# A third of the convolution on GpSimd during attention, the large gate halves on VectorE, the convolution's norm at the seventh gate and its columns ahead of the last gate's third product

## The chip, the cores and the metric

The kernel runs on one core of one Trainium2 chip. The metric is the device time of one execution in microseconds (us); lower is better. The engines are named as the profile names them: PE is TensorE (PEld its weight loads), DVE is VectorE, ACT is ScalarE, POOL is GpSimd, SP is SyncE, which here only issues loads.

## The reference, cut to what matters

Two layers of a trunk run on 512 latent and 128 context tokens, all in fp32. In each layer a normalised input `u` is projected to q, k, v, to the input of a convolution module, and to two gates. Attention and convolution are two branches, merged by the gates:

```python
proj = u @ w_in
q, k, v, a_glu, gates = jnp.split(proj, ...)
attn_br = block_attention(q, keys, vals) @ w_attn_o
ga, gb = jnp.split(a_glu, 2, axis=-1)
cv = depthwise_conv(ga * jax.nn.sigmoid(gb), conv_w, conv_b)      # 31 taps, 512 channels
cv = jax.nn.silu(layernorm(cv, conv_ln_g, conv_ln_b))
conv_br = cv @ w_conv_o
gate_a, gate_c = jnp.split(gates, 2, axis=-1)
merged = jax.nn.sigmoid(gate_a) * attn_br + jax.nn.sigmoid(gate_c) * conv_br
h = h + g1 * (merged @ w_out)
```

A mixture of 16 experts follows in each layer, then the next layer.

## The kernel before, in words

Every engine has its own program, written out in order; semaphores tie them together, and nothing reorders the work. Both layers run the same loop body, so each stage stands twice in the trace.

Products are exact to fp32 by splitting: a number is written as a high half (rounded, type fp32r) and a low half (the rest), and each product is three passes on PE, high x high, high x low, low x high. For a weight tile that SP has loaded into `raw`, ACT writes the high half `w_hi` (function `hi`, L1097) and POOL subtracts it to get the low half `w_lo` (function `lo` of GpSimd, L2261). There are two slots of each; a tile is 128 x 2048 or 128 x 1024.

Tokens stand in 640 columns. The stages of a layer around the change are:

* GLU: the input of the convolution, `glu`, four chunks of 128 channels by 700 columns (pads included). It ends before attention.
* Attention: 16 heads, taken in pairs. For each pair DVE computes the inverse row sums (`rinv`, L1667), POOL spreads them into `rrow` (L2301, function `inverse_row`), and PE turns them (L615, function `inverse_rows`) one pair of heads later. POOL also sends three rows of the modulation to memory (`modulation`, `bias`), and has nothing else there.
* Gates: eight gates (`b8` 0 to 7). Each has three products of 48 matmuls of 320 columns: `gta` and `gtc` (both from one tile of 128 x 2048, the "large half" below is its `w_lo`) and `ao` (the attention output, a tile of 128 x 1024), all at L534. ACT takes the sigmoids of the first two (`sga` L1315, `sgc` L1321), DVE multiplies `ao` by `sga` into `m_t` (L1843). Beside this DVE runs the convolution: 31 taps by four chunks, 124 instructions of 128 x 670, four TENSOR_SCALAR (L1832) and 120 SCALAR_TENSOR_TENSOR (L1835), 21 per gate in gates 0 to 4 and 19 in gate 5, going round the four chunks, so that an instruction depends on the fourth one before it. They stand in DVE's program ahead of the two `m_t` of their gate.
* The convolution's norm: ahead of gate 7 PE transposes the convolution to tokens (L711, `conv_tokens`), DVE takes mean and variance and writes `cn` (L1810 to L1822, `conv_norm`), and ACT takes a square root between. After gate 7 PE transposes `cn` back to channels (L734), ACT applies SiLU (L1331) and takes the high half (L1333), DVE the low half `c_lo` (L1857).
* co: the product with `w_conv_o` (L534 again, 192 matmuls), which waits for the last `c_lo`; DVE merges it (L1870, L1873) and splits the result (`m_lo`, L1861); the product with `w_out` (L791) waits for the last `m_lo`.

Of the kernel before, what the change touches and what calls it, by code (L numbers as in the profile page):

```python
# [164 lines left out]
def _build(nc, io, out, ledger, ctx):  # L165
# [64 lines left out]
    cv = at("cv", [P, CCH, CO], F32, R_A + 60 * KB)  # L230
# [66 lines left out]
    n1row = at("n1row", [P, 512], F32, R_W + 20 * KB)  # L297
# [67 lines left out]
    wrow = routed("wrow", [P, 1], F32)  # L365

# [63 lines left out]
    def _(eng):  # L430
# [37 lines left out]
        with eng.Fori(0, DEPTH) as l:  # L468
# [235 lines left out]
            def conv_tokens():  # L704

                eng.wait_ge(*T.at("cv"))
                for t in range(NT):
                    b = fill(("cvT", t))
                    c0 = t * P if t < LT else CTX0
                    for c in range(CCH):  # L710
                        ins = nc.tensor.transpose(ps[:, b, c * P:(c + 1) * P], cv[:, c, c0:c0 + P], ident[:, :])  # L711
                    ins.then_inc(*T.filled(("cvT", t)))


            for b8 in range(KC):
# [12 lines left out]

            eng.wait_ge(*T.at("cn"))
            for c in range(CCH):  # L730
                for part, tiles in ((0, range(LT)), (1, (LT,))):
                    b = fill(("cT", c, part))
                    for i, t in enumerate(tiles):
                        ins = nc.tensor.transpose(ps[:, b, i * P:(i + 1) * P], cn[:, t, c * P:(c + 1) * P], ident[:, :])  # L734
                    ins.then_inc(*T.filled(("cT", c, part)))
# [339 lines left out]
    def _(eng):  # L1075
# [8 lines left out]
        with eng.Fori(0, DEPTH) as l:  # L1084
# [220 lines left out]

            for b8 in range(KC):
                if b8 == KC - 1:
# [17 lines left out]
            for c in range(CCH):
                if c >= 2:
                    eng.wait_ge(*A.at("c_lo", c - 2))
                for part, (c0, n) in enumerate(((0, NLAT), (NLAT, P))):
                    eng.wait_ge(*A.at("filled", ("cT", c, part)))
                    b = A.bank(("cT", c, part))  # L1330
                    act(c_f[:, c % 2, c0:c0 + n], ps[:, b, 0:n], ACT.Silu, bias=lnb[:, c:c + 1], scale=lng[:, c:c + 1]).then_inc(*A.drained(("cT", c, part)))  # L1331
                eng.wait_ge(*A.at("drained", ("cT", c, 1)))
                act(c_hi[:, c, :], c_f[:, c % 2, :], ACT.Copy).then_inc(*A.up("a_c", "c_hi", c))  # L1333
# [106 lines left out]
    def _(eng):  # L1440
# [30 lines left out]
        with eng.Fori(0, DEPTH) as l:  # L1471
            V.l = l

            def lo(n):

                eng.wait_ge(*V.at("w_hi", n))
                if n < U_MOE:
# [5 lines left out]
                    v.tensor_tensor(w_of(n, 0), raw[:, n % 2, :], w_of(n, 1).bitcast(F32), ALU.subtract).then_inc(*V.up("v_lo", "w_lo", n))  # L1483
# [317 lines left out]
            taps = [(k, c) for k in range(TAPS) for c in range(CCH)]  # L1801
            tap_step = {}
            share = -(-len(taps) // (KC - 2))
# [23 lines left out]

            for b8 in range(KC):
                for k, c in taps[b8 * share:(b8 + 1) * share]:
                    src = glu[:, c, k:k + CO]  # L1830
                    if k == 0:
                        ins = v.tensor_scalar(cv[:, c, :], src, convw[:, c, 0:1], convb[:, c:c + 1], ALU.mult, ALU.add)  # L1832
                    else:
                        eng.wait_ge(*V.at("v", tap_step[(k - 1, c)]))
                        ins = v.scalar_tensor_tensor(out=cv[:, c, :], in0=src, scalar=convw[:, c, k:k + 1], in1=cv[:, c, :],  # L1835
                                                     op0=ALU.mult, op1=ALU.add)
                    ins.then_inc(*V.step())
                    tap_step[(k, c)] = V.steps
# [5 lines left out]
                if b8 == KC - 2:  # L1844
                    ALIAS(("cv",), ("v", tap_step[(TAPS - 1, CCH - 1)]))
                    conv_norm()
# [330 lines left out]
    def _(eng):  # L2177
# [70 lines left out]
        with eng.Fori(0, DEPTH) as l:  # L2248
# [76 lines left out]
            for n in range(U_GATE + 2, U_MOE):  # L2325
                lo(n)
# [138 lines left out]
```

## Time and profile before

| | us |
|---|---|
| median of 3 runs (1926.95 to 1933.87) | 1927.54 |
| the profiled execution's own time | 1929.48 |
| its span, first to last instruction | 1927.6 |
| busy PE / DVE / POOL | 1581.1 / 1257.6 / 616.8 |
| mean granted TensorE clock, as a share of full speed | 0.909 |

All rows come from the one profiled execution; it took 1.9 us more than the median. A busy PE is not PE at its peak: matmuls are pipelined, and a matmul of 320 columns that is listed with 0.31 us starts 0.147 us after the one before. Where rows say "x2" or more, instructions that follow each other closely are put in one row. What stands in brackets at a row's end is the idle time of the engine before it, and whom it waited for.

### The profile page before, as it was taken

To read this page: it belongs to the slowest core of one execution; us is meant where nothing else is said; L and a number is where in the kernel's file an instruction comes from. 1 tells how busy PE (TensorE), PEld (TensorE's weight loads), DVE (VectorE), ACT (ScalarE), POOL (GpSimd) and SP (SyncE) were. 2 spreads that over 40 slices of the span, in tenths; PEclk is the share of its full clock that TensorE was granted. 3 is DMA by queue.
4 is the path that set the end of the run, shared out by engine and by line. 5 is a ranking of instruction groups with operands and counts; after the bars stand their busy time and mean duration, and the time that the engine had idled before them with its cause. 6 is when DMAs were issued, how large, how long until landed. Compare 5 with 4: busy or idle time off the path is not lost.

```text
span 1927.6 us, 26921 instructions
## 1 busy us (share of the span) xinstructions
PE 1581.1 (82%) x8954; PEld 1352.6 (70%) x8954; DVE 1257.6 (65%) x1728; ACT 785.0 (41%) x1178; POOL 616.8 (32%) x298
## 2 busy tenths in 40 slices
PE   2799899879998894999649989998899889399970
PEld 0589766669998673777538976667899878377750
DVE  0658588888844454778284948887984355568735
ACT  0413477731123131666142247775111322266621
POOL 2123100053322210789312320003333221059941
PEclk7799899989998895999869999999999989599995
DMA  7513165222221615799862205541222162569976
GB/s 280 195 44 93 52 210 179 78 57 65 69 64 47 259 74 187 276 357 366 300 214 71 66 29 197 187 132 34 66 67 66 45 239 70 221 227 363 369 290 228
DMA packets 131202, 310.02 MB, mean 161 GB/s; under 512 B 11636, under 2 KB 81396, under 8 KB 109984
## 3 DMA queue, kind: packets, MB, share of 16 engines
q1 hardware_dynamic: 104096, 224.41, 33.9%
q0 software_dynamic: 16400, 42.90, 6.1%
q10 hardware_dynamic: 10560, 40.90, 5.6%
q8 instruction: 76, 1.25, 0.3%
q14 instruction: 70, 0.57, 0.1%
HBM read 287.06 MB, written 39.44 MB: 169 GB/s over the span
## 4 chain that ended last, share of the span: by engine, by line
PE 50%; issue 16%; DMA 13%; DVE 11%; POOL 6%; ACT 4%; DVEq 0%; ACTq 0%; POOLq 0%; SPq 0%
PE ps L534 15%; PE ps L493 9%; PE ps L791 6%; POOL w_lo L2261 4%; PE ps L592 3%; DMA raw<-in_w_down 3%; PE ps L602 2%; DVE gu_lo L1485 2%; PE ps L449 2%; DMA raw_x<-in_w_down 2%; DMA raw<-in_w_ada 2%; PE ps L857 2%; PE ps L581 2%; PE ps L837 1%; DMA raw_x<-in_w_up 1%
## 5 line engine op out<-in xcount | busy, mean ns | idle before, releaser
L2261 POOL TENSOR_TENSOR w_lo<-raw,w_hi 128x2048 fp32r<-128x2048 f32 (+1 forms) x60 | 259.9, 4336 | 516.7 <-ACT w_hi L1097 516.5
L534 PE MATMUL ps<-u_hi,w_hi 128*128 128x320 f32 x768 | 245.5, 320 | 35.4 <-POOL w_lo L2261 29.7
L534 PE MATMUL ps<-u_lo,w_hi 128*128 128x320 f32 x768 | 242.6, 316 | 0.0
L534 PE MATMUL ps<-u_hi,w_lo 128*128 128x320 f32 x768 | 242.4, 316 | 0.0
L1835 DVE SCALAR_TENSOR_TENSOR cv<-glu,convw,cv 128x670 f32<-128x670 f32 x240 | 235.8, 1057 | 0.0
L1097 ACT ACTIVATE w_hi<-raw 128x2048 fp32r<-128x2048 f32 (+1 forms) x64 | 101.3, 1591 | 310.2 <-PE ps L534 151.1
L534 PEld LDWEIGHTS ps<-u_hi,w_hi 128*128 128x128 f32 x768 | 149.1, 194 | 39.1 <-issue 16.7
L534 PEld LDWEIGHTS ps<-u_lo,w_hi 128*128 128x128 f32 x768 | 149.5, 195 | 0.1
L534 PEld LDWEIGHTS ps<-u_hi,w_lo 128*128 128x128 f32 x768 | 149.0, 194 | 0.0
L2340 POOL DMA_INDIRECT xe<-u_d,tab_u x34 | 77.7, 2286 | 179.4 <-issue 145.7
L1700 DVE TENSOR_TENSOR pt_lo<-ps,pt_hi 128x512 fp32r<-128x512 f32 x160 | 109.7, 687 | 31.2 <-ACT pt_hi L1222 29.1
L1661 DVE TENSOR_REDUCE nmax<-ps 128x1 f32<-128x640 f32 x128 | 104.0, 815 | 27.6 <-PE ps L582 25.9
L1196 ACT ACTIVATE probs<-ps,nmax 128x640 f32<-128x640 f32 x128 | 101.4, 793 | 49.6 <-DVE nmax L1661 47.1
L592 PEld LDWEIGHTS ps<-ident,probs 128*128 128x128 f32 x640 | 77.6, 144 | 62.2 <-issue 32.8
L1222 ACT ACTIVATE pt_hi<-ps 128x512 fp32r<-128x512 f32 x160 | 94.8, 594 | 54.2 <-PE ps L592 46.2
L592 PE MATMUL ps<-ident,probs 128*128 128x128 f32 x640 | 102.3, 284 | 17.0 <-DVE pt_lo L1700 9.1
L837 PE MATMUL ps<-gu_hi,xt_hi 128*128 128x512 f32 x240 | 96.8, 403 | 19.9 <-DVE xt_lo L2091 19.8
L2301 POOL COPY rrow<-rinv 128x512 f32<-128x512 f32 x16 | 9.8, 613 | 295.7 <-DVE rinv L1667 295.7
L837 PE MATMUL ps<-gu_lo,xt_hi 128*128 128x512 f32 x240 | 94.0, 392 | 0.0
L837 PE MATMUL ps<-gu_hi,xt_lo 128*128 128x512 f32 x240 | 93.5, 389 | 0.0
L581 PE MATMUL ps<-k_hi,q_st 128*128 128x320 f32 x256 | 85.3, 342 | 5.1 <-DVE q_st L1631 1.7
L791 PE MATMUL ps<-w_hi,m_hi 128*128 128x512 f32 x160 | 65.8, 411 | 18.3 <-DVE m_lo L1861 18.3
(372 smaller groups left out, 4121.1 us busy)
## 6 DMA issues: line engine op xcount, KB each, us to landing
raw<-in_w_ada SPq DMA_DIRECT2D x52, 1024.0 KB, 5.0
raw<-in_w_in SPq DMA_DIRECT2D x48, 512.0 KB, 5.0
raw_x<-in_w_gate SPq DMA_DIRECT2D x16, 1024.0 KB, 6.1
raw<-in_w_up SPq DMA_DIRECT2D x16, 1024.0 KB, 8.3
raw_x<-in_w_down SPq DMA_DIRECT2D x16, 1024.0 KB, 9.4
raw_x<-in_w_up SPq DMA_DIRECT2D x14, 1024.0 KB, 8.5
raw<-in_w_gate SPq DMA_DIRECT2D x14, 1024.0 KB, 6.8
raw<-in_w_down SPq DMA_DIRECT2D x14, 1024.0 KB, 8.9
```

The source lines that it names most:

```text
L493: ins = mm(ps[:, b, :], (u_hi, u_lo)[x][:, k, t * P:(t + 1) * P], w_of(n, 1 - w)[:, c * 512:(c + 1) * 512], start=(k == 0 and w + x == 0), ...
L534: ins = mm(ps[:, b, 0:HALF], (w_hi, w_lo)[w][:, s, cols(k):cols(k) + P], xs[x][:, k, half * HALF:(half + 1) * HALF], start=(k == 0 and w + ...
L581: mm(ps[:, b, 0:HALF], q, k_hi[:, g, i * HALF:(i + 1) * HALF], start=True, stop=False)
L592: ins = nc.tensor.transpose(ps[:, b, t * P:(t + 1) * P], probs[:, h % 2, t, kc * P:(kc + 1) * P], ident[:, :])
L791: ins = mm(ps[:, t, :], (m_hi, m_lo)[x][:, k, t * P:(t + 1) * P], (w_hi, w_lo)[w][:, s, c * 512:(c + 1) * 512], start=(k == 0 and w + x == ...
L837: ins = mm(ps[:, 2, :], (xt_hi, xt_lo)[x][:, k, :], (gu_hi, gu_lo)[w][i][:, k, :], start=(k == 0 and w + x == 0), stop=(k == 7 and w == 1))
L1097: act(w_of(n, 1)[:, 0:k], raw[:, n % 2, 0:k], ACT.Copy).then_inc(*A.up("a_hi", "w_hi", n))
L1196: ins = act(probs[:, h % 2, t, :].rearrange("p (a b) -> p a b", a=2), ps[:, b0:b0 + 2, 0:HALF], ACT.Exp, bias=nmax[:, h % 2, t:t + 1], acc ...
L1661: v.tensor_reduce(nmax[:, h % 2, t:t + 1], ps[:, b0:b0 + 2, 0:HALF], axis=AX.XY, op=ALU.max, negate=True).then_inc(*V.up("v_max", "nmax", ...
L1700: v.tensor_tensor(pt_lo[:, k, :], ps[:, b, :], pt_hi[:, k, :].bitcast(F32), ALU.subtract).then_inc(*V.drained(("PT", h, kc)))
L1835: ins = v.scalar_tensor_tensor(out=cv[:, c, :], in0=src, scalar=convw[:, c, k:k + 1], in1=cv[:, c, :], op0=ALU.mult, op1=ALU.add)
L2261: g_.tensor_tensor(w_lo[:, n % 2, 0:k], raw[:, n % 2, 0:k], w_hi[:, n % 2, 0:k].bitcast(F32), ALU.subtract).then_inc(*G.up("g_lo", "w_lo", n))
```

## The change

It has four parts. (1) The taps go chunk by chunk now. The first 40 (31 of chunk 0, nine of chunk 1) run on POOL during attention, between the spreads of the row sums; POOL has no fused form, so a tap is a product into `tap_tmp` and an addition, each waiting for the one before. The other 84 stay on DVE in gates 0 to 5 (8, 15, 15, 15, 16 and 15), and each waits for the tap before it. Chunk 0 has a tile of its own, chunks 1 to 3 are written over the input of the chunk before. (2) The large halves of gates 1 to 7 are computed by DVE, after the taps of the gate before; POOL keeps the small ones. (3) `conv_tokens` and `conv_norm` stand at gate 6. (4) The transposes of `cn` stand in gate 7 between `gtc` and `ao`, ACT's SiLU after the high half of the next tile, and DVE's `c_lo` ahead of the last two `m_t`. Besides, a memset of 128 rows becomes one of 64, and DVE's function `lo` takes the tile's size.

```diff
+    cvs = [cv0[:, :]] + [glu[:, c, 0:CO] for c in range(CCH - 1)]
+    POOL_TAPS = 40
+    tap_list = [(c, k) for c in range(CCH) for k in range(TAPS)]
...
             for b8 in range(KC):
-                if b8 == KC - 1:
+                if b8 == 6:
                     conv_tokens()
...
                 feature_rows([("gtc", b8, i) for i in range(2)], s, lambda k: k * 256 + 128, KC, (u_hi, u_lo))
+                if b8 == KC - 1:
+                    conv_columns()
...
-                if b8 == KC - 1:
+                if b8 == 6:
                     eng.wait_ge(*A.at("cv_var"))
...
                 hi(gate_units(b8)[0] + 2)
+                if b8 == KC - 1:
+                    silu_columns()
                 hi(gate_units(b8)[1] + 2)
...
+            taps = tap_list[POOL_TAPS:]
+            bounds = [round(len(taps) * x / 5.5) for x in (0, 0.5, 1.5, 2.5, 3.5, 4.5, 5.5)]
...
             for b8 in range(KC):
-                for k, c in taps[b8 * share:(b8 + 1) * share]:
+                for c, k in taps[bounds[b8]:bounds[b8 + 1]] if b8 < 6 else ():
...
-                        eng.wait_ge(*V.at("v", tap_step[(k - 1, c)]))
+                        eng.wait_ge(*V.at("v", V.steps))
...
+                if b8 < KC - 1:
+                    lo(gate_units(b8 + 1)[0])
+                else:
+                    c_lows()
                 for i in range(2):
                     eng.wait_ge(*V.at("filled", ("ao", b8, i)))
...
-                if b8 == KC - 2:
+                if b8 == 5:
                     conv_norm()
...
+            def conv_taps(count):
+                for c, k in itertools.islice(taps, count):
+                    if k == 0:
...
+                    else:
+                        eng.wait_ge(*G.at("tap", c, k - 1))
+                        g_.tensor_tensor(tap_tmp[:, :], glu[:, c, k:k + CO], convw[:, c, k:k + 1].broadcast_to([P, CO]), ALU.mult).then_inc(*G.up("g_tap", "product", c, k))
+                        eng.wait_ge(*G.at("product", c, k))
+                        ins = g_.tensor_tensor(cvs[c], cvs[c], tap_tmp[:, :], ALU.add)
+                    ins.then_inc(*G.up("g_tap", "tap", c, k))
...
+            conv_taps(10)
             inverse_row(0)
+            conv_taps(6)
             inverse_row(1)
             modulation(1)
             bias(0, DEPTH - 1 - l)
-            inverse_row(2)
-            inverse_row(3)
+            for h2 in range(2, 4):
+                conv_taps(6)
+                inverse_row(h2)
             modulation(2)
             for h2 in range(4, 7):
+                conv_taps(6)
                 inverse_row(h2)
...
-            for n in range(U_GATE + 2, U_MOE):
+            for b8 in range(1, KC):
+                lo(gate_units(b8)[1])
+            for n in range(U_CO, U_MOE):
                 lo(n)
```

On POOL, at the start of attention, before: the bias loads, and then one spread (`rrow`) after the other.

```order
L2183 DMA adab<-in_b_ada 4x512 x2
L2299 ISA
L2301 COPY rrow<-rinv 128x512
L2299 REGISTER_ALU
L2301 COPY rrow<-rinv 128x512
L2217 ISA
```

The same place after the change (`cv_209` is the tile of chunk 0):

```order
L2201 DMA adab<-in_b_ada 4x512 x2
L2312 ISA
L2316 TENSOR_SCALAR cv_209<-glu,convw,convb 128x670
L2318 ISA
L2319 TENSOR_TENSOR tap_tmp<-glu,convw 128x670
L2320 REGISTER_ALU
L2321 TENSOR_TENSOR cv_209<-cv_209,tap_tmp 128x670
...
L2336 ISA
L2338 COPY rrow<-rinv 128x512
```

Ten taps (19 instructions) stand ahead of the first spread, and six (12 instructions) ahead of each of the second to the sixth, until the 40 are used up.

On DVE, at the end of a gate's taps, before: taps, the two products of the gate, and the next gate's taps.

```order
L1835 SCALAR_TENSOR_TENSOR cv<-glu,convw,cv 128x670
L1840 REGISTER_ALU
L1842 REGISTER_ALU
L1843 TENSOR_TENSOR m_t<-ps,sga 128x320
L1840 REGISTER_ALU
L1842 REGISTER_ALU
L1843 TENSOR_TENSOR m_t<-ps,sga 128x320
L1834 REGISTER_ALU
L1835 SCALAR_TENSOR_TENSOR cv<-glu,convw,cv 128x670
```

The same place after the change (the taps of chunks 1 to 3 write into `glu`):

```order
L1853 SCALAR_TENSOR_TENSOR glu<-glu,convw 128x670
L1488 REGISTER_ALU
L1496 TENSOR_TENSOR w_lo<-raw,w_hi 128x2048
L1863 REGISTER_ALU
L1865 REGISTER_ALU
L1866 TENSOR_TENSOR m_t<-ps,sga 128x320
L1863 REGISTER_ALU
L1865 REGISTER_ALU
L1866 TENSOR_TENSOR m_t<-ps,sga 128x320
L1852 REGISTER_ALU
L1853 SCALAR_TENSOR_TENSOR glu<-glu,convw 128x670
```

The large half of the next gate's tile has come between the taps and the products.

On PE, at the end of gate 7, before: the transposes of `cn` stand after `ao` and ahead of co.

```order
L534 MATMUL ps<-o_hi,w_lo 128x320
L729 REGISTER_ALU
L438 REGISTER_ALU
L734 MATMUL ps<-ident,cn 128x128 x4
...
L734 MATMUL ps<-ident,cn 128x128
L749 REGISTER_ALU
L438 REGISTER_ALU
L534 MATMUL ps<-c_hi,w_hi 128x320
```

The same transposes after the change:

```order
L539 MATMUL ps<-u_hi,w_lo 128x320
L721 REGISTER_ALU
L443 REGISTER_ALU
L726 MATMUL ps<-ident,cn 128x128 x4
...
L726 MATMUL ps<-ident,cn 128x128
L740 REGISTER_ALU
L443 REGISTER_ALU
L539 MATMUL ps<-o_hi,w_hi 128x320
```

They stand between `gtc` and `ao` of gate 7 now, so that `ao` comes between them and co.

## Rows read from the trace of the kernel before

**Rows 1.** Gates and norm: us; busy PE, PEld, DVE, ACT, POOL; PE clock; DMA.
```profile
399.40:603.28 203.88, 180.65 (x1195) 178.84 (x1194) 145.96 (x175) 53.70 (x74) 73.73 (x19) 0.95 0.22 61
```

**Rows 2.** Chain that ended last: start us, us, what; gate 6, transposes, gate 7, co.
```profile
547.87 21.38 PE ps L534 x144
569.24 2.18 PE ps L711 x20
571.43 21.14 PE ps L534 x144
...
603.28 13.03 PE ps L534 x72
```

**Rows 3.** Whom PE waited for, gates and norm: us, times, longest; layer 0, layer 1.
```profile
PE ps L534 <- POOL w_lo L2261: 14.5, 4, 7.9
PE ps L534 <- DVE c_lo L1857: 8.5, 1, 8.5
...
PE ps L534 <- POOL w_lo L2261: 15.2, 5, 7.9
```

**Rows 4.** Timeline of DVE, gate 2: start us, us, engine, line, instruction.
```profile
453.06 19.61 DVE L1835 SCALAR_TENSOR_TENSOR cv<-glu,convw,cv 128x670 f32<-128x670 f32 x21
```

**Rows 5.** The tile cv: nanoseconds of one tap, least, median, most.
```profile
L1835 DVE SCALAR_TENSOR_TENSOR cv<-glu,convw,cv x240: 899/905/4353, 410.1 to 1468.4; 128x670 f32<-128x670 f32 x120
```

**Rows 6.** Timeline of POOL, end of attention and first gates.
```profile
390.39 4.53 POOL L2261 TENSOR_TENSOR w_lo<-raw,w_hi 128x2048 fp32r<-128x2048 f32 x1 [8.47 <-ACT w_hi L1097]
398.89 2.39 POOL L2261 TENSOR_TENSOR w_lo<-raw,w_hi 128x1024 fp32r<-128x1024 f32 x1
416.10 12.55 POOL L2261 TENSOR_TENSOR w_lo<-raw,w_hi 128x2048 fp32r<-128x2048 f32 x1 [13.26 <-ACT w_hi L1097]
453.70 2.53 POOL L2261 TENSOR_TENSOR w_lo<-raw,w_hi 128x1024 fp32r<-128x1024 f32 x1 [1.19 <-ACT w_hi L1097]
```

**Rows 7.** Timeline of DVE, start of a layer, merge, and a dependent pair.
```profile
985.93 2.29 DVE L1483 TENSOR_TENSOR w_lo<-raw,w_hi 128x2048 fp32r<-128x2048 f32 x1 [2.02 <-issue]
...
671.14 0.68 DVE L1905 TENSOR_TENSOR h_a<-ps,g_row 128x512 f32<-128x512 f32 x1
671.86 0.69 DVE L1907 TENSOR_TENSOR h_a<-h_a,h_in 128x512 f32<-128x512 f32 x1
...
630.16 4.74 DVE L1861 TENSOR_TENSOR m_lo<-m_t,m_hi 128x640 fp32r<-128x640 f32 x1 [0.77 <-ACT m_hi L1339]
636.55 0.82 DVE L1861 TENSOR_TENSOR m_lo<-m_t,m_hi 128x640 fp32r<-128x640 f32 x1
```

**Rows 8.** Timeline of ACT, gates 6 and 7 and the SiLU's table.
```profile
541.13 1.91 ACT L1097 ACTIVATE w_hi<-raw 128x2048 fp32r<-128x2048 f32 x1
585.54 0.44 ACT L1321 ACTIVATE sgc<-ps 128x320 f32<-128x320 f32 x1 [3.08 <-PE ps L534]
585.88 1.05 ACT L1097 ACTIVATE w_hi<-raw 128x1024 fp32r<-128x1024 f32 x1
593.66 1.28 ACT L1331 ACT_TABLE_LOAD   x1
```

**Rows 9.** Timeline of attention, POOL and PE: bias loads, first and sixth spread, their use.
```profile
220.22 2.21 POOL L2183 DMA_DIRECT2D adab<-in_b_ada  x4
248.83 0.61 POOL L2301 COPY rrow<-rinv 128x512 f32<-128x512 f32 x1 [26.39 <-DVE rinv L1667]
356.15 0.61 POOL L2301 COPY rrow<-rinv 128x512 f32<-128x512 f32 x1 [20.08 <-DVE rinv L1667]
...
266.92 0.60 PE L615 MATMUL ps<-ident,rrow 128*128 128x128 f32 x4
375.75 0.60 PE L615 MATMUL ps<-ident,rrow 128*128 128x128 f32 x4
```

**Rows 10.** DVE in attention: two splits beside POOL; the normalisation of context rows.
```profile
391.90 1.29 DVE L1700 TENSOR_TENSOR pt_lo<-ps,pt_hi 128x512 fp32r<-128x512 f32 x2 [2.60 <-ACT pt_hi L1222]
...
L1691 DVE TENSOR_TENSOR ctxp<-ctxp,csum x8: 691/691/693, 236.0 to 1293.0; 128x512 f32<-128x512 f32 x8
```

More of the change, by code:

```diff
@@ L710, in conv_tokens, with conv_columns @@
                     for c in range(CCH):
-                        ins = nc.tensor.transpose(ps[:, b, c * P:(c + 1) * P], cv[:, c, c0:c0 + P], ident[:, :])
+                        ins = nc.tensor.transpose(ps[:, b, c * P:(c + 1) * P], cvs[c][:, c0:c0 + P], ident[:, :])
                     ins.then_inc(*T.filled(("cvT", t)))
+            def conv_columns():
+                eng.wait_ge(*T.at("cn"))
+                for c in range(CCH):
+                    for part, tiles in ((0, range(LT)), (1, (LT,))):
+                        b = fill(("cT", c, part))
+                        for i, t in enumerate(tiles):
+                            ins = nc.tensor.transpose(ps[:, b, i * P:(i + 1) * P], cn[:, t, c * P:(c + 1) * P], ident[:, :])
+                        ins.then_inc(*T.filled(("cT", c, part)))
             for b8 in range(KC):
-                if b8 == KC - 1:
+                if b8 == 6:
                     conv_tokens()
@@ L726, in _ @@
                 feature_rows([("ao", b8, i) for i in range(2)], s, lambda k: k * P, KC, (o_hi, o_lo))
[L729 to L735, printed above, removed]
             eng.wait_ge(*T.at("c_lo", CCH - 1))
@@ L1304, in _, with silu_columns @@
                 act(o_hi[:, k, :].rearrange("p (t n) -> p t n", t=NT), o_t[:, :, k, :], ACT.Copy).then_inc(*A.up("a_oh", "o_hi", k))
+            def silu_columns():
+                for c in range(CCH):
+                    if c >= 2:
+                        eng.wait_ge(*A.at("c_lo", c - 2))
+                    for part, (c0, n) in enumerate(((0, NLAT), (NLAT, P))):
+                        eng.wait_ge(*A.at("filled", ("cT", c, part)))
+                        b = A.bank(("cT", c, part))
+                        act(c_f[:, c % 2, c0:c0 + n], ps[:, b, 0:n], ACT.Silu, bias=lnb[:, c:c + 1], scale=lng[:, c:c + 1]).then_inc(*A.drained(("cT", c, part)))
+                    eng.wait_ge(*A.at("drained", ("cT", c, 1)))
+                    act(c_hi[:, c, :], c_f[:, c % 2, :], ACT.Copy).then_inc(*A.up("a_c", "c_hi", c))
             for b8 in range(KC):
-                if b8 == KC - 1:
+                if b8 == 6:
                     eng.wait_ge(*A.at("cv_var"))
@@ L1322, in _ @@
                 hi(gate_units(b8)[0] + 2)
+                if b8 == KC - 1:
+                    silu_columns()
                 hi(gate_units(b8)[1] + 2)
[L1325 to L1333, printed above, removed]
             for j in range(N_CO):
@@ L1482, in lo @@
                         eng.wait_ge(*V.at("mod_out", "first"))
-                    v.tensor_tensor(w_of(n, 0), raw[:, n % 2, :], w_of(n, 1).bitcast(F32), ALU.subtract).then_inc(*V.up("v_lo", "w_lo", n))
+                    k = size(n)
+                    v.tensor_tensor(w_of(n, 0)[:, 0:k], raw[:, n % 2, 0:k], w_of(n, 1)[:, 0:k].bitcast(F32), ALU.subtract).then_inc(*V.up("v_lo", "w_lo", n))
                     return
@@ L1800, in _ @@
             eng.wait_ge(*V.at("v", k_pad))
-            taps = [(k, c) for k in range(TAPS) for c in range(CCH)]
-            tap_step = {}
-            share = -(-len(taps) // (KC - 2))
+            eng.wait_ge(*V.at("tap", *tap_list[POOL_TAPS - 1]))
+            taps = tap_list[POOL_TAPS:]
+            bounds = [round(len(taps) * x / 5.5) for x in (0, 0.5, 1.5, 2.5, 3.5, 4.5, 5.5)]
             def conv_norm():
@@ L1854, in _ @@
             ALIAS(("wr_a",), ("v", V.steps))
-            for c in range(CCH):
-                eng.wait_ge(*V.at("c_hi", c))
-                v.tensor_tensor(c_lo[:, c, :], c_f[:, c % 2, :], c_hi[:, c, :].bitcast(F32), ALU.subtract).then_inc(*V.up("v_c", "c_lo", c))
             def m_lo_of(b8):
```

30 lines of the change are left out of this document (22 added, 8 removed).

## The prediction, made before the changed kernel ran

> **What bounds the kernel now.** I looked first at busy time by stage, then at the chain that ended last, then at whom PE waits for, and last at the timelines of DVE and POOL in the same stretch. The stage that the change touches most, from the first gate matmul to the first matmul of co, lasts 203.9 us in layer 0 at a granted clock of 0.95 [rows 1]. An undisturbed gate shows in the chain: 144 matmuls in 21.14 us [rows 2], 0.147 us each. Eight of them are 169.1 us. The rest is waiting, and the list of waits names two causes: PE waits 14.5 us (15.2 in layer 1) for POOL's low halves and 8.5 us for the last `c_lo` [rows 3].
>
> The timelines say why POOL is late. Alone, it takes 4.53 us for a low half of 2048 columns; the one at 416.10 took 12.55 [rows 6]. In that stretch DVE ran taps without a break, each at its usual 0.905 us [rows 5]. So POOL stood still until DVE made a pause, and then DVE stood still: a tap took up to 4.35 us [rows 5]. With 21 taps a gate costs DVE 19.6 us in its taps [rows 4], nearly the 21.14 us that PE needs, so the pauses are rare. Gates 6 and 7, which have no taps, run at PE's pace.
>
> How much of the 203.9 us is stall? From the end of gate 7's `gtc` (its last sigmoid starts at 585.54, rows 8) to co at 603.28 [rows 2] are 17.74 us. Without stalls the stage would be 169.1 - 7.05 (the `ao` third of gate 7, which lies inside the 17.74) + 2.18 (transposes, rows 2) + 17.74 = 182.0. The stall in the gates is 203.9 - 182.0 = 21.9 us: the 14.5 that are listed, and slower matmuls after a stop (as at co's start, below) and waits that the list misses.
>
> **The large halves and the taps, gates 0 to 5.** DVE has 15 taps per gate (8 in gate 0, 16 in gate 4) where it had 21. A tap now waits for the one before. What such a wait costs DVE is shown by a dependent pair: 671.14 + 0.68 = 671.82, and the next starts at 671.86 [rows 7], 0.04 us. So a tap is 0.905 + 0.04 = 0.945 us and 15 are 14.2. POOL's small half falls into them and may hold DVE for its 2.39 us [rows 6]. The two `m_t` of the gate before end about 0.5 us after the gate begins. Taps end at 0.5 + 14.2 + 2.4 = 17.1 us into the gate. The tile's high half is ready at 14.1 (end of `gtc`) + 0.4 + 1.9 [rows 8] = 16.5, so it isn't late. DVE's low half takes 2.29 us [rows 7] and is done at 19.4 (20.3 in gate 4). PE wants it at 21.14. It waits for nothing, with 0.8 to 1.8 us to spare; the whole 21.9 us go. Bounds: nothing is gained if DVE needs the same 24 us a gate as now (0), and no more than the stall can go (-21.9). I take -21.9, as the sum for DVE holds even with the POOL block counted in full.
>
> What is queued behind the new wait on DVE is the gate's own `m_t`, whose PSUM bank PE needs eight fills later; the next gate's sigmoids on ACT wait for it, and PE doesn't wait for those for another gate's third. The next loads into the freed slot go out at 19 us and have 17 us until ACT wants them. Both are covered.
>
> **The norm at gate 6.** `conv_tokens` waits for tap 84. By the sum above the taps end 17 us into gate 5, 4 us ahead of PE. The transposes cost PE the same 2.18 us as before [rows 2], and the norm lies beside gate 6 instead of gate 7: 0. If the taps were late, every us of it would be one on PE.
>
> **The columns in gate 7.** Before, the SiLU's table load starts at 593.66 [rows 8], after `ao`, and co starts 9.62 us later at 603.28 [rows 2]. Now the chain starts as soon as ACT has written its next high half, at 585.88 + 1.05 = 586.93 [rows 8]. The first transposes are out by then. That is 6.7 us sooner. `ao` (7.05 us) must fit in between: its first bank is freed by the first chunk's SiLU, about 3.5 us after the end of `gtc`, so it ends 10.6 after it, and the last `c_lo` 11 after it. The two end together. -6.7, between 0 (if `ao` is held to the end) and -8.5, the listed wait [rows 3].
>
> **co.** PE starts co from a stop, and its first 72 matmuls take 13.03 us [rows 2], 0.181 each instead of 0.147: 2.5 us. Without the stop this goes. Its end is set by DVE's `m_lo`, which POOL's last two tiles still hold up (4.74 us for 0.82, rows 7). -2.5, bounds -3.5 and 0.
>
> **The taps on POOL.** Not shown before: a product and a sum of 670 columns on POOL. Its low half of 1024 takes 2.39 us and of 2048 takes 4.53 [rows 6], so 2.09 ns a column and 0.25 fixed: 1.65 us for 670. With 0.04 for the wait, 1.69; two TENSOR_SCALAR at about 0.8 (the spread of 512 columns takes 0.61, rows 9). A layer has 76 x 1.69 + 1.6 = 130 us. It starts when the bias loads are out, at 222.43 [rows 9]. Ten taps end at 254, and the first spread ends near 254.5 instead of 249.4; PE uses it at 266.92 [rows 9]. The sixth spread comes after all 40: 222.4 + 130 + 3.7 (six spreads) + 3.3 (three pairs of loads at 1.1) = 359.5; PE uses it at 375.75 [rows 9]. 16 us to spare, and the spreads between have 12 to 15. An instruction could take 1.90 us before PE waited. From the contended end of the rows (12.55 us for 2048 columns) one would be 4.1; but those taps on DVE had two SBUF inputs, and in attention DVE reads PSUM. I take 1.69, and 0 on the path.
>
> Does POOL slow DVE there? Two splits of PSUM at 391.90 took 1.29 together beside POOL's low half [rows 6, 10], undisturbed. Only the normalisation of the context rows has both inputs in SBUF: 8 of 0.69 us in the trace [rows 10], three per layer beside taps. Each may wait for up to one POOL instruction, 1.65 us. +1.2 a layer (half), bounds 0 and +5.
>
> **Sum.** Layer: -21.9 - 6.7 - 2.5 + 1.2 = -29.9. Layer 1 has the same stalls (15.2 for 14.5, rows 3): together -60. Against the execution's own 1929.5 that is 1870; that execution stood 1.9 above the median of 1927.5, which gives 1868. I say 1870.
>
> **A rule that bears on this.** Taps (two SBUF inputs) and POOL's halves exclude one another: 12.55 us against 4.53 for POOL, 4.74 against 0.82 for `m_lo` [rows 6, 7]. The Trainium skill, page "SBUF — State Buffer", section "Who interferes with whom", says that the shared port pair is an exclusive lock and that whoever issues first has it for the whole instruction. The exclusion agrees with the rows. The turn doesn't: by the rule POOL at 416.10 would have waited for one tap, and it waited 8 us, through ten. With the rule the gates come out as in my sum; if the row's manner holds for the new taps, it is the first rival.
>
> **Rivals.** *DVE's taps still shut POOL out.* Now POOL's small half would be pushed behind the taps: they end at 0.5 + 14.2 = 14.7, the half at 17.1, and PE wants it for `ao` at 14.1: 3 us in five gates and two layers, 30 us, so 1900. For it: 416.10. Against it: the half at 453.70 got in among taps (2.53, rows 6), and the new taps have a pause of 0.04 after each. 0.12.
>
> *DVE becomes the gates' pace.* If a dependent tap cost 1.1 us or more, a gate would take 22 to 23 us instead of 21.14: +1 to +2 in five gates, two layers, 1880 to 1890. Against it: the pair in rows 7. 0.10.
>
> *POOL overruns attention.* At x us an instruction the sixth spread is 76 (x - 1.90) late, PE waits, and all behind it shifts. The change breaks even at 29.9/76 above, x = 2.29; at 2.6, the kernel is at about 1870 + 2 x 53 = 1976, slower than before. For it: the product reads its weight with a stride of zero, which no POOL row of two inputs does, and a POOL row went as far as 12.55. Against it: the spread, also read with a stride of zero, takes 0.61 for 512 columns. 0.06, of which 0.04 on the slower side.
>
> **How the numbers follow.** The forecast has 0.72. Its own range is 1862 to 1882, from the bounds of co, the columns and the context rows. To hold 8 in 10 the range takes in the second rival and most of the first: 1858 to 1894. A measurement of this kernel can tell 0.5% from no change, 9.6 us. Faster by more than that: 0.72 + 0.12 + 0.10 less a little for what I don't see, 0.92; within it 0.03; slower 0.05.
>
> **What would show it.** Right: the gates without waits of PE for a low half; POOL's taps near 1.65 us an instruction, the spreads after them ready ahead of PE; co starting about 29 us nearer to the first gate matmul. Wrong: PE waiting for `rrow` in attention, for `w_lo` of a small tile ahead of `ao`, or for the convolution at gate 6.

## The result, and the profile after

The changed kernel takes 1873.06 us (median of 4 runs, 1871.83 to 1877.71), the kernel before, run beside it, 1927.24: a ratio of 0.9721, 95% interval 0.9688 to 0.9753. The forecast was 1870 us. The profiled execution of the changed kernel has a span of 1870.7 us, where before had 1927.6: 56.9 us shorter, against 60 predicted. The two medians are 54.2 us apart.

The stage from the first gate matmul to co, layer 0 and layer 1 (columns as in [rows 1]: us; busy PE, PEld, DVE, ACT, POOL; granted clock; DMA share):

```profile
396.25:571.66 175.41, 173.83 (x1195) 173.32 (x1194) 126.51 (x137) 52.81 (x74) 22.89 (x11) 1.00 0.24 68
1296.76:1472.17 175.41, 173.83 (x1195) 173.32 (x1193) 126.52 (x137) 52.82 (x74) 22.90 (x11) 1.00 0.24 68
```

It was 203.88 us [rows 1], so 28.5 are gone (27.6 of 203.0 in layer 1), and the two layers now take the same time. PE has the same 1195 records, but they take 173.8 us instead of 180.7 [rows 1]. The granted clock is 1.00 throughout, its level of 2.4 GHz; before, it was 0.95 on the mean, in a stage where PE stood still several times.

The chain that ended last, over the same stage (start us, us, what):

```profile
396.50 126.72 PE ps L539 x864
523.21 2.18 PE ps L716 x20
525.39 35.21 PE ps L539 x240
...
562.03 1.28 ACT L1322
563.33 0.79 ACT c_f L1322
564.15 7.31 PE ps L539 x48
571.46 0.20 issue
571.66 10.82 PE ps L539 x72
```

Six gates are one piece of 864 matmuls, 21.12 us a gate; after the transposes come gate 6 and two thirds of gate 7, 240 matmuls in 35.21, the same pace. Before, such pieces stood there for gates 6 and 7 [rows 2]. Whom PE waited for there, layer 0 (layer 1 reads the same):

```profile
PE ps L539 <- ACT c_f L1322: 1.4, 1, 1.4
PE ps L539 <- DVE c_lo L1844: 0.2, 1, 0.2
PE ps L620 <- POOL rrow L2338: 0.2, 1, 0.2
```

The 14.5 us for POOL's low halves and the 8.5 for `c_lo` [rows 3] have gone. What is left is 1.4 us for the first bank of `ao`, which the first chunk's SiLU frees. ACT at that place, the last sigmoid and the SiLU's table (timeline, as in [rows 8]):

```profile
560.63 0.44 ACT L1341 ACTIVATE sgc<-ps 128x320 f32<-128x320 f32 x1 [3.08 <-PE ps L539]
560.96 1.05 ACT L1106 ACTIVATE w_hi<-raw 128x1024 fp32r<-128x1024 f32 x1
562.03 1.28 ACT L1322 ACT_TABLE_LOAD   x1
```

DVE and POOL in gate 2 (start us, us, engine, line, instruction; in brackets the idle time before and whom it waited for):

```profile
439.26 16.28 DVE L1853 SCALAR_TENSOR_TENSOR glu<-glu,convw 128x670 f32<-128x670 f32 x15
455.47 2.28 DVE L1496 TENSOR_TENSOR w_lo<-raw,w_hi 128x2048 fp32r<-128x2048 f32 x1
...
439.90 2.54 POOL L2279 TENSOR_TENSOR w_lo<-raw,w_hi 128x1024 fp32r<-128x1024 f32 x1 [18.67 <-ACT w_hi L1106]
```

Fifteen taps take 16.3 us where 21 took 19.6 [rows 4]. DVE's low half for gate 3 is done at 457.75; gate 3 starts at 396.50 + 3 x 21.12 = 459.86. POOL's small half asks just after the first tap and is through in 2.54 us, close to its undisturbed 2.39 [rows 6].

POOL's taps, first the two kinds with their least, median and most nanoseconds (both layers; of the sums those of chunk 0), then the timeline of the first taps and of two spreads:

```profile
L2319 POOL TENSOR_TENSOR tap_tmp<-glu,convw x76: 1293/1303/1638, 221.7 to 1249.6; 128x670 f32<-128x670 f32 x76
L2321 POOL TENSOR_TENSOR cv<-cv,tap_tmp x60: 1601/1622/1958, 223.1 to 1221.5; 128x670 f32<-128x670 f32 x60
```

```profile
221.68 1.30 POOL L2319 TENSOR_TENSOR tap_tmp<-glu,convw 128x670 f32<-128x670 f32 x1
223.06 1.61 POOL L2321 TENSOR_TENSOR cv<-cv,tap_tmp 128x670 f32<-128x670 f32 x1
224.75 1.30 POOL L2319 TENSOR_TENSOR tap_tmp<-glu,convw 128x670 f32<-128x670 f32 x1
...
249.61 0.61 POOL L2338 COPY rrow<-rinv 128x512 f32<-128x512 f32 x1
...
353.02 0.61 POOL L2338 COPY rrow<-rinv 128x512 f32<-128x512 f32 x1 [1.07 <-DVE rinv L1680]
```

A tap is 224.75 - 221.68 = 3.07 us. The first spread, behind ten taps, starts at 249.61 and is used at 263.36; the sixth, behind all 40, starts at 353.02 after waiting for DVE, and PE takes it at 372.61:

```profile
263.36 0.60 PE L620 MATMUL ps<-ident,rrow 128*128 128x128 f32 x4
372.61 0.60 PE L620 MATMUL ps<-ident,rrow 128*128 128x128 f32 x4
```

In co and its merge little has changed beyond the faster start (72 matmuls in 10.82 us in the chain above, for 13.03 in [rows 2]). POOL's two tiles of `w_out` still hold DVE up, as they did in `m_lo`'s row of [rows 7], and PE waits 9.1 us between co and `w_out`, as before. DVE's timeline, and the list of PE's waits:

```profile
596.33 4.74 DVE L1879 TENSOR_TENSOR m_lo<-m_t,m_hi 128x640 fp32r<-128x640 f32 x1 [0.77 <-ACT m_hi L1351]
604.46 4.12 DVE L1891 TENSOR_TENSOR m_t<-m_t,m_tmp 128x640 f32<-128x640 f32 x1
```

```profile
PE ps L800 <- DVE m_lo L1879: 9.1, 1, 9.1
```

The normalisation of the context rows on DVE, 8 times 0.69 us before [rows 10], now takes up to 1.92 us at a time beside POOL's taps:

```profile
L1704 DVE TENSOR_TENSOR ctxp<-ctxp,csum x8: 691/1443/1924, 233.4 to 1263.5; 128x512 f32<-128x512 f32 x8
```

### The profile page after: what moved, and what is told of

It is laid out like the page before. It is cut to its first block, busy times and chain, and to the rows that moved or that the text cites. A ratio compares the mean times of both kernels' runs of the same rounds, so it can differ in the third digit from the quotient of the medians.

```text
span 1870.7 us, 27095 instructions
## 1 busy us (share of the span) xinstructions
PE 1565.5 (84%) x8954; PEld 1338.9 (72%) x8954; DVE 1221.8 (65%) x1662; ACT 785.7 (42%) x1178; POOL 738.5 (39%) x440
## 4 chain that ended last, share of the span: by engine, by line
PE 62%; DMA 14%; DVE 11%; issue 7%; ACT 4%; POOL 1%; DVEq 0%; ACTq 0%; POOLq 0%; SPq 0%
PE ps L539 26%; PE ps L498 9%; PE ps L800 6%; PE ps L597 3%; PE ps L607 2%; DVE gu_lo L1498 2%; DMA raw_x<-in_w_down 2%; PE ps L454 2%; DMA raw<-in_w_down 2%; PE ps L866 2%; DMA raw<-in_w_up 2%; PE ps L586 2%; DMA raw<-in_w_ada 2%; PE ps L846 2%; PE ps L587 1%
## 5 line engine op out<-in xcount | busy, mean ns | idle before, releaser
L2279 POOL TENSOR_TENSOR w_lo<-raw,w_hi 128x1024 fp32r<-128x1024 f32 (+1 forms) x46 | 162.5, 3535 | 554.9 <-ACT w_hi L1106 554.9
L539 PE MATMUL ps<-u_hi,w_hi 128*128 128x320 f32 x768 | 238.9, 311 | 5.4 <-ACT probs L1205 5.4
L539 PE MATMUL ps<-u_lo,w_hi 128*128 128x320 f32 x768 | 238.1, 310 | 0.0
L539 PE MATMUL ps<-u_hi,w_lo 128*128 128x320 f32 x768 | 238.1, 310 | 0.0
L1853 DVE SCALAR_TENSOR_TENSOR glu<-glu,convw 128x670 f32<-128x670 f32 x164 | 171.1, 1043 | 6.1 <-DVE o_lo L1808 0.6
L539 PEld LDWEIGHTS ps<-u_hi,w_hi 128*128 128x128 f32 x768 | 144.8, 189 | 6.0 <-ACT probs L1205 5.9
L539 PEld LDWEIGHTS ps<-u_lo,w_hi 128*128 128x128 f32 x768 | 144.8, 189 | 0.1
L2384 POOL DMA_INDIRECT xe<-u_d,tab_u x34 | 68.4, 2012 | 179.6 <-issue 145.2
L2319 POOL TENSOR_TENSOR tap_tmp<-glu,convw 128x670 f32<-128x670 f32 x76 | 100.0, 1316 | 5.3
L2321 POOL TENSOR_TENSOR cv<-cv,tap_tmp 128x670 f32<-128x670 f32 x60 | 98.3, 1639 | 4.7
```

Source lines behind the costliest of these rows:

```text
L539: ins = mm(ps[:, b, 0:HALF], (w_hi, w_lo)[w][:, s, cols(k):cols(k) + P], xs[x][:, k, half * HALF:(half + 1) * HALF], start=(k == 0 and w + ...
L1853: ins = v.scalar_tensor_tensor(out=cvs[c], in0=glu[:, c, k:k + CO], scalar=convw[:, c, k:k + 1], in1=cvs[c], op0=ALU.mult, op1=ALU.add)
L2279: g_.tensor_tensor(w_lo[:, n % 2, 0:k], raw[:, n % 2, 0:k], w_hi[:, n % 2, 0:k].bitcast(F32), ALU.subtract).then_inc(*G.up("g_lo", "w_lo", n))
```

## The experiments

Ratios are to runs of the kernel before on the same chip: its median was 1927 to 1930 us beside all of them. "Stage" is the time from the first gate matmul to co in layer 0: 203.9 us before, 175.4 in the change.

**All taps back on VectorE.** The rest of the change stays.

```diff
-            POOL_TAPS = 40
+            POOL_TAPS = 0
...
```

> Undoes the first part alone: all 124 taps are on DVE again, 11 in gate 0 and 22 or 23 in each of gates 1 to 5, one waiting for the other; the large halves, the norm and the columns stay as changed. If DVE's port time sets the gates, a gate needs 22.5 taps of 0.955 us + 2.4 (POOL's small half between them) + 2.3 (large half) + 0.9 (products) = 27 us on DVE against 21.1 on PE: +30 us a layer, about 1935 us. If the gain came from taking the large halves off POOL, the time stays within 10 us of 1873.

Measured: 1926.07 us, ratio 0.9987 (0.9973 to 1.0). The whole gain is gone, though every low half, norm and column of the change is still in place. Stage: about 202.5 us. PE's waits there:

```profile
PE ps L539 <- DVE w_lo L1496: 15.2, 3, 7.2
PE ps L716 <- DVE glu L1852: 5.3, 1, 5.3
```

The stall has only moved from POOL's `w_lo` to DVE's. With 22 taps (20.91 us), a low half (2.28) and its two products a gate takes DVE 23.8 us; POOL's small halves come on top, two of them in every second gate, which then takes 28.4 to 28.8. PE needs 21.1.

```profile
449.59 20.91 DVE L1852 SCALAR_TENSOR_TENSOR glu<-glu,convw 128x670 f32<-128x670 f32 x22
470.41 2.28 DVE L1496 TENSOR_TENSOR w_lo<-raw,w_hi 128x2048 fp32r<-128x2048 f32 x1
```

The theory put the time 9 us too high, with the right mechanism. The rival (taking the large halves off POOL does it) falls.

**The large halves back on POOL.** The taps stay shared.

```diff
-                if b8 < KC - 1:
-                    lo(gate_units(b8 + 1)[0])
-                else:
+                if b8 == KC - 1:
                     c_lows()
...
-            for b8 in range(1, KC):
-                lo(gate_units(b8)[1])
-            for n in range(U_CO, U_MOE):
+            for n in range(U_GATE + 2, U_MOE):
                 lo(n)
```

> Undoes the second part alone: the large halves of gates 1 to 7 go back to POOL. If what delayed POOL was the unbroken stream of DVE's taps, POOL starts 16.5 us into the gate, waits for one tap at most and takes 4.53: done at 21.1 to 22 against PE's 21.1, so 0 to +6 us a layer, 1873 to 1885. If POOL's share of the port is itself what cost the 14.5 us of waits, those waits come back: +29 us or more, from 1902.

Measured: 1880.25 us, ratio 0.9762 (0.9734 to 0.979), which overlaps the change's interval. Stage: 178.3 us, 2.9 more than the change. With fewer taps DVE is through with them, or in the last, when POOL asks for a large half, and POOL is hardly held:

```profile
437.45 4.62 POOL L2277 TENSOR_TENSOR w_lo<-raw,w_hi 128x2048 fp32r<-128x2048 f32 x1 [13.06 <-ACT w_hi L1106]
...
458.89 4.62 POOL L2277 TENSOR_TENSOR w_lo<-raw,w_hi 128x2048 fp32r<-128x2048 f32 x1 [13.04 <-ACT w_hi L1106]
```

The two stand 458.89 - 437.45 = 21.44 us apart, 0.32 more than PE's 21.12 for a gate: POOL's half now ends a little after PE wants it. So moving the large halves is worth some 3 us of the stage once the taps are shared, within the first theory's 0 to 6, and not a term of the size of the stall.

**The large halves alone, put into the kernel before.**

```diff
...
+                if b8 < KC - 1:
+                    lo(gate_units(b8 + 1)[0])
...
-            for n in range(U_GATE + 2, U_MOE):
+            for b8 in range(1, KC):
+                lo(gate_units(b8)[1])
+            for n in range(U_CO, U_MOE):
                 lo(n)
```

> The kernel before with the second part alone: DVE computes the large halves of gates 1 to 7 between its taps and its products, all 124 taps stay on DVE in their old order. DVE needs 17.4 us for 21 taps, 2.4 for POOL's small half, 0.9 and 2.3: 23 us a gate against 21.1. So about half of the 21.9 us of stalls a layer goes: about 1905. If the large halves on POOL were the whole cause, all of it goes: 1883.

Measured: 1909.73 us, ratio 0.9883 (0.9848 to 0.9917). Stage: 194.4 us, 9.5 less than before. The theory holds, with a gain of 20 us where it said 24: without the shared taps the stall shrinks and PE still waits.

```profile
PE ps L534 <- DVE w_lo L1484: 8.8, 4, 5.8
PE ps L534 <- DVE c_lo L1860: 8.6, 1, 8.6
```

**The columns back behind gate 7.** `conv_columns` after the loop on PE, `silu_columns` after it on ACT, `c_lows` after the router's rows on DVE.

```diff
-                if b8 == KC - 1:
-                    conv_columns()
...
+            conv_columns()
             eng.wait_ge(*T.at("c_lo", CCH - 1))
...
-                if b8 == KC - 1:
-                    silu_columns()
                 hi(gate_units(b8)[1] + 2)
+            silu_columns()
...
```

> Undoes the fourth part alone: the transposes of the normalised convolution, the SiLU and the low halves stand behind gate 7 again. By the prediction's step a layer loses 6.7 us at the start of co and about 2 us in co, whose first matmuls then run after a stop: +17 us, 1890. If ao hides nothing, the time stays at 1873.

Measured: 1886.27 us, ratio 0.9785 (0.9757 to 0.9813), 13 us above the change. Stage: 182.1 us (+6.7). PE waits again, as in [rows 3], and co starts from a stop:

```profile
PE ps L539 <- DVE c_lo L1843: 8.6, 1, 8.6
```

From the start of co to that of `w_out` it takes 1.5 us more in layer 0 and 2.8 in layer 1. These two are the prediction's terms of 6.7 and 2.5, by themselves. Over two layers they make 17.7 us, and the time shows 13; the rest lies behind `w_out`, where traces of one and the same program differ by as much (see the sum, below).

**Each product of POOL's taps computed twice.**

```diff
+                        g_.tensor_tensor(tap_tmp[:, :], glu[:, c, k:k + CO], convw[:, c, k:k + 1].broadcast_to([P, CO]), ALU.mult).then_inc(*G.up("g_tap", "product0", c, k))
+                        eng.wait_ge(*G.at("product0", c, k))
                         g_.tensor_tensor(tap_tmp[:, :], glu[:, c, k:k + CO], convw[:, c, k:k + 1].broadcast_to([P, CO]), ALU.mult).then_inc(*G.up("g_tap", "product", c, k))
```

> The changed kernel with each product of POOL's taps computed twice (the second writes the same values). A tap then takes 1.30 + 1.30 + 1.62 + 3 x 0.08 = 4.46 us instead of 3.08, and the sixth spread of the row sums is ready at 399 us in layer 0 instead of 353, where PE wanted it at 373. If the slack is what the prediction says, PE waits in attention for what exceeds it: about +26 us a layer, 1926. If the spreads' lateness is absorbed elsewhere, less.

Measured: 1923.24 us, ratio 0.9962 (0.9947 to 0.9977). The added 38 x (1.30 + 0.08) = 52 us of POOL a layer use up the slack, the sixth spread's 19 us ahead of PE and 4.6 for which POOL waited for DVE, and then cost PE the rest: co starts 28.0 us later than in the change in layer 0 and 26 more in layer 1. The cause shows at the spreads, where PE had never waited more than 0.2 us (waits of PE in attention, layer 0, and the sixth spread with its use):

```profile
PE ps L620 <- POOL rrow L2340: 21.9, 6, 9.5
```

```profile
399.69 0.61 POOL L2340 COPY rrow<-rinv 128x512 f32<-128x512 f32 x1
...
400.35 0.66 PE L620 MATMUL ps<-ident,rrow 128*128 128x128 f32 x4 [3.47 <-POOL rrow L2340]
```

The stage itself stays at 175.4. So the third rival's mechanism is real, and the change stands some 24 us of POOL's work a layer away from it.

**Do the pauses let POOL in?** Two kernels ask. In the first, DVE's taps go round the chunks again (two of them in a tile of their own), so that no tap waits for the one just before it.

```diff
-    cvs = [cv0[:, :]] + [glu[:, c, 0:CO] for c in range(CCH - 1)]
+    cv23 = at("cv23", [P, 2, CO], F32, R_A + 60 * KB)
+    cvs = [cv0[:, :], glu[:, 0, 0:CO], cv23[:, 0, :], cv23[:, 1, :]]
...
-            taps = tap_list[POOL_TAPS:]
+            left = [[ck for ck in tap_list[POOL_TAPS:] if ck[0] == c] for c in (1, 2, 3)]
+            taps = [x[r] for r in range(TAPS) for x in left if r < len(x)]
...
```

> The changed kernel with DVE's 84 taps taken in turn over chunks 1 to 3, as the kernel before did over four, so that a tap doesn't wait for the one before it and there is no pause of 0.04 us between taps. 15 taps then take 12.5 us instead of 14.3. If a stream without pauses shuts POOL out, POOL's small half starts only when the taps end, 13 us into the gate, is done at 15.4 against PE's 14.2, and PE waits 1.2 us in five gates a layer: +12 us, 1885. If the port goes to whoever asks first, POOL waits for one tap at most, PE waits for nothing and the time is 1873.

Measured: 1875.03 us, ratio 0.9707 (0.9672 to 0.9742), not to be told from the change. Stage: 175.4. POOL isn't shut out. But it asks at the one moment that the change leaves it, within a tap of the start of the stream, and so this run doesn't settle what happens amid it:

```profile
443.83 0.91 DVE L1856 SCALAR_TENSOR_TENSOR cv<-glu,convw,cv 128x670 f32<-128x670 f32 x1
444.66 3.07 DVE L1856 SCALAR_TENSOR_TENSOR glu<-glu,convw 128x670 f32<-128x670 f32 x1
...
444.48 2.53 POOL L2283 TENSOR_TENSOR w_lo<-raw,w_hi 128x1024 fp32r<-128x1024 f32 x1 [18.68 <-ACT w_hi L1107]
```

The second has all 124 taps on DVE, each waiting for the one before, and all low halves of the gates on POOL, so that POOL asks amid the taps as it did at 416.10 of before.

```diff
-            POOL_TAPS = 40
+            POOL_TAPS = 0
...
-            for b8 in range(1, KC):
-                lo(gate_units(b8)[1])
-            for n in range(U_CO, U_MOE):
+            for n in range(U_GATE + 2, U_MOE):
                 lo(n)
```

> All 124 taps on VectorE, chunk by chunk, each waiting for the tap before it, and all low halves of the gates on GpSimd. It asks whether the pause of 0.04 us after each tap lets GpSimd in. Theory (the pause lets it in): wherever GpSimd asks amid the taps, a half of 2048 columns takes 4.53 + at most 0.95 = 5.5 us, and the tap that meets it some 5 us. Rival (taps that follow each other closely shut GpSimd out, pause or not): in gate 0 the half asked for at about 416 takes 8 us or more, as the 12.55 us before the change. Time: VectorE needs 124 x 0.955 = 118 us of taps and loses about 5 + 2.5 us a gate to GpSimd, some 40 us, so the convolution is ready about 160 us after 408, or 568, where the transposes could start at 528: about 1873 + 2 x 40 = 1953 us by the theory; by the rival GpSimd's halves come late besides, 1960 or more. The place decides, not the time.

Measured: 1946.5 us (one run), 19 us slower than the kernel before. DVE has been in its taps for 8 us when POOL asks at 411.44 and has its 2048 columns in 4.73 us, where it had 12.55 [rows 6] (the list of DVE starts at 405):

```profile
405.03 12.80 DVE L1852 SCALAR_TENSOR_TENSOR cv<-glu,convw,cv 128x670 f32<-128x670 f32 x9
...
411.44 4.73 POOL L2276 TENSOR_TENSOR w_lo<-raw,w_hi 128x2048 fp32r<-128x2048 f32 x1 [13.24 <-ACT w_hi L1106]
```

All twelve such halves amid taps, six a layer, take 4.62 to 5.07 us. So where each tap waits for the one before, with its 0.04 us, POOL gets in within one tap, and the first rival's mechanism falls for taps of this kind. DVE then pays for both (a tap takes up to 5.2 us) and is the pace: PE waits 23.2 us for the convolution ahead of gate 6, and 9.7 for low halves.

**The low halves of `w_out` on VectorE.** In the changed kernel POOL's two tiles hold DVE at 596.33 and 604.46 (above).

```diff
             for b8 in range(KC):
+                if b8 == 6:
+                    lo(U_OUT)
...
             m_lo_of(KC - 1)
+            lo(U_OUT + 1)
...
-            for n in range(U_CO, U_MOE):
+            for n in itertools.chain(range(U_CO, U_OUT), range(U_OUT + 2, U_MOE)):
                 lo(n)
```

> The changed kernel with two more tiles moved from POOL to DVE: the low halves of the first two tiles of w_out, the first after the fifth merge, the second after the last m_lo. In the trace of the changed kernel POOL's two tiles hold up DVE's m_lo (4.74 us for 0.82) and m_t (4.12 for 0.83) at the end of co, while DVE would need 2.29 us for a tile. If these blocks set the start of the w_out product, it starts about 4.4 us a layer earlier: 1864. If something else sets it, 1873.

Measured: 1877.03 us, ratio 0.973 (0.9706 to 0.9754). A miss. `w_out` does start 4.7 us sooner after co (4.4 us of wait for 9.1), and PE then loses more than that inside it:

```profile
PE ps L800 <- DVE h_a L1926: 8.6, 1, 8.6
PE ps L800 <- DVE m_lo L1879: 4.4, 1, 4.4
```

`h_a` clears PE's banks, but stands on DVE behind two operations on `a_row`, which wait for a row of memory, `n_row`, and were then held by a POOL half as well. The load of `n_row` went out 6.4 us sooner than in the change, at 611.06 for 617.5, but took 25.9 us to land where it had taken 17.6:

```profile
636.97 6.66 DVE L1911 SCALAR_TENSOR_TENSOR a_row<-a_row,n_row 128x1024 f32<-128x1024 f32 x2 [28.33 <-DMA n_row<-in_norm_g]
643.55 0.68 DVE L1926 TENSOR_TENSOR h_a<-ps,g_row 128x512 f32<-128x512 f32 x1
```

**The same, with `h_a` ahead of the rows that come last.** `g_row` and `h_in` get a semaphore of their own, and the two operations on `a_row` follow the first five `h_a`.

```diff
...
-            eng.wait_ge(*V.at("n2_in"))
+            eng.wait_ge(*V.at("h_in"))
             eng.wait_ge(*V.at("m_lo", KC - 1))
-            for i in range(2):
-                v.scalar_tensor_tensor(out=a2_row[:, i, :], ...
...
             for nh in range(2):
                 cols = slice(nh * 512, (nh + 1) * 512)
+                if nh:
+                    eng.wait_ge(*V.at("n2_in"))
+                    for i in range(2):
+                        v.scalar_tensor_tensor(out=a2_row[:, i, :], ...
```

> The change with the low halves of both w_out tiles on VectorE, as in the experiment on them, and besides VectorE clears the first half of the w_out product before it touches the row that comes last from memory: h_a waits for g_row and h_in alone, and the two operations on a_row and n_row stand after the first five h_a. Theory: what took the gain of the earlier start was the wait for n_row (landed at 636.97) with the tensor product full in PSUM, 8.6 us of PE; h_in lands some 15 us after its issue at 607.4, about 623, before the first bank is full. So w_out starts 4 us earlier than in the change and PE doesn't wait in it: about 1873 - 2 x 4 = 1865 us. Rival (the gain is given back further on, in the experts, as 2 us of the change's own gain were): 1870 to 1874.

Measured: 1856.48 us (5 runs, 1852.23 to 1860.75), ratio 0.9632 (0.9613 to 0.965). The unaltered change beside it:

> The changed kernel itself, unaltered, on the same chip and beside the same runs of before, so that the version above can be set against it: 1871 to 1878 us by every theory.

Measured: 1870.27 us (6 runs, 1868.0 to 1878.46), ratio 0.9701 (0.9688 to 0.9715). The intervals are apart, so this version beats both kernels, by 13.8 us against the change where 8 were expected. The wait inside `w_out` is gone (list of PE's waits, then DVE's timeline):

```profile
PE ps L800 <- DVE m_lo L1879: 4.4, 1, 4.4
```

```profile
626.28 0.69 DVE L1927 TENSOR_TENSOR h_a<-ps,g_row 128x512 f32<-128x512 f32 x1 [16.14 <-PE ps L800]
```

`w_out` starts 4.7 us sooner after co than in the unaltered change's trace, in both layers, and PE doesn't lose it again inside. At the start of the routing behind it 7.5 us are gained in layer 0 and another 5.2 in layer 1; what goes beyond the 4.7 lies within what the stretch from `w_out` to the routing differs by among traces with the same program there (99 to 102 us). The two spans differ by more, 1876.9 and 1858.7, but that execution of the change was the slowest of its six. Some 3 us of the difference lie in the experts of layer 0, a stretch in which the twelve traces of this case, all with the same program there, differ by 3.3 us; they are no gain that a run shows.

## Why the prediction was right

**The gates.** From the first gate matmul to the last sigmoid of gate 7 it took 585.54 - 399.40 = 186.1 us; now it takes 560.63 - 396.25 = 164.4. That is -21.8 for a forecast of -21.9 (-20.9 in layer 1), and the experiments show the step as it was argued: DVE's account per gate decides. A tap has a pitch of 0.955 us (0.945 assumed; the prediction added 0.04 for the wait to the listed 0.905, but taps that don't wait start every 0.83 us, so the wait costs 0.12), POOL's small half held a tap for some 2.0 us of the 2.4 allowed, and in gate 2 the low half was ready 2.1 us ahead of PE (1.8 forecast for a gate of 15 taps). The prediction gave the 21.9 to "the large halves and the taps" together. The runs divide them: the halves alone take 9.5 off the stage; the taps on POOL, with the columns' 6.7, take 203.9 - 178.3 = 25.6 off, so about 19 without the columns; halves beside taps that wait for each other and all stay on DVE bring nothing (a stage of 202.5, with the columns moved). They overlap, and the taps carry it.

Of the 28.5, 180.65 - 173.83 = 6.8 us appear as shorter PE records, at a granted clock of 1.00 for 0.95. The prediction had this within its 21.9, as the part that the list of waits misses, and for co as a term of its own.

**The norm at gate 6.** Forecast 0. PE's list has no wait for the convolution there. No run undoes this part alone; where the taps come late, PE does wait at that place (5.3 us with all taps on DVE, 23.2 with the low halves on POOL besides).

**The columns.** From the last sigmoid to co it is now 571.66 - 560.63 = 11.0 us, for 17.7: -6.7, as forecast, also in the working: `ao` begins 3.5 us after the end of `gtc`, ends 10.9 after it (10.6 forecast), and the last `c_lo` makes PE wait 0.2 us more. Taken back by itself, the step costs 6.7.

**co.** Its first 72 matmuls went from 13.03 to 10.82 us, -2.2; in layer 1 the whole of co is 1.5 shorter. The forecast of -2.5 was a little high.

**POOL's taps.** Estimated 1.69 us an instruction, product and sum alike. The sum is 1.62 + 0.08, the product 1.30 + 0.08. A tap is 3.07 instead of 3.38, and the sixth spread came at 353.6 instead of 359.5, although POOL had waited 4.6 us for DVE by then. The estimate erred to the safe side: the wait is twice the 0.04 taken over from DVE, and the product is 0.35 cheaper than the sum that it was priced as. What it rests on held: the spreads have 13 to 20 us to spare, and with 52 us more work on POOL the loss per layer is 26 to 28, where the break-even working gives 76 x (2.23 - 1.90) = 25 (2.23 us is an instruction's share with the second product). A tap takes POOL two instructions in every trace here; no run tries another form.

**The context rows, +1.2.** The mechanism shows on DVE: their normalisation takes 5.2 us in layer 0 and 5.3 in layer 1 instead of 2.8, so DVE loses 2.5 us a layer beside the taps. What PE loses by it is too small for two traces: from the end of the last product ahead of attention to the first gate matmul it took 182.8 us before and 181.6 in the change, and in layer 1 it grew by 1.1. Over all traces the mean is 181.4 us in the four kernels without taps on POOL and 182.7 in seven executions with the 40 taps (the run with the product twice left out): +1.3, though single ones lie between 180.4 and 185.5.

**The sum.** -28.5 and -27.6 for the stages and -2.2 and -1.5 for co make 30.7 and 29.1 us in the two layers; the prediction had 21.9 + 6.7 + 2.5 = 31.1 for these. The profiled execution ended 56.9 us earlier and not 59.8. The experts of layer 0 took 337.5 us in it and 334.8 before, with nothing changed there; the twelve traces have 334.3 to 337.6. So the last 3 us are within what one execution differs from another. The prediction's own range, 1862 to 1882, has a slip: its lower end takes all bounds together, and its upper end by the same working is 1896. The time lies inside either.

**The rule on the shared port.** The Trainium skill, page "SBUF — State Buffer", section "Who interferes with whom", lets whoever issues first have the pair for its whole instruction. With a pause after each tap the runs agree: POOL waits for one tap at most (4.73 us for 4.53), and a tap then waits for POOL (up to 5.2 us). With taps that follow without a pause the rows and the rule still differ, and not at 416.10 alone. In the trace of before nine large halves, over both layers, asked amid such a stream; each stood for 1.0 to 8.0 us (its time less the undisturbed 4.53), until the stream's last tap had ended. In the run with the halves alone a small half stood 4.4 us, through three taps and DVE's own low half behind them:

```profile
420.05 6.77 POOL L2264 TENSOR_TENSOR w_lo<-raw,w_hi 128x1024 fp32r<-128x1024 f32 x1 [19.13 <-ACT w_hi L1097]
```

POOL did get in behind the first tap of a stream. The half at 453.70, which the prediction held against the first rival, had asked 0.64 us after the stream's start, as had those of the run without pauses (0.64 to 0.74 us, all ten done in 2.44 to 2.54 us); so that row says nothing on what happens later in a stream. That the pause makes the difference follows from the traces together, in which the taps' order, their number per gate and their tiles differ too; no run changes the pause alone for a half that asks amid the taps. Why the first tap lets POOL in and the later ones don't is open.

## What to carry to other kernels

Add up what each engine must do in one round of the loop, at its measured pitch and with the time that a shared port takes from it, and compare it with PE's round: moving work between two engines that exclude one another (the large halves) pays in full only while the receiver's sum stays below PE's; moving it into a stage where the receiver is idle (the taps into attention) pays as long as the receiver's own deadlines hold, here the spreads with some 24 us a layer. When a wait is taken away, look next at what the freed engine meets: the earlier `w_out` gained nothing until the operation that waits for the last row from memory no longer stood ahead of the ones that free PE's banks.

## What the runs showed of the hardware

A product on POOL whose second operand is one column read with a stride of zero took 1.30 us for 670 columns; a sum of two full operands took 1.62, and the first tap of a chunk, a TENSOR_SCALAR, 0.91. A dependent instruction starts 0.08 us after its predecessor's end on POOL (221.68 + 1.30 to 223.06), 0.04 on DVE. On DVE, taps that don't wait start every 0.83 us though each is listed with 0.90 (443.83, 444.66), and taps that wait every 0.955: the wait costs 0.12 us a tap, and in the gates of this kernel nothing, as DVE has that time (a stage of 175.4 us with and without it).

In a stream of taps without waits POOL's subtraction got in behind the first tap or when the stream was over, and at no tap between; with a wait of each tap for the one before it got in behind the tap that was running.
